# A transformer pair on one core: the router's product on four column groups, high parts multiplied before low parts behind each norm, weight splits and root tables moved out of the norms

## The chip, the cores and the metric

The kernel runs on one core of a Trainium2 chip. The core has a matrix engine (TensorE, PE in the profile; its weight loads are PEld), a vector engine (VectorE, DVE), a scalar engine with function tables (ScalarE, ACT), a general engine (GpSimd, POOL) and a sync engine that issues transfers (SyncE, SP). The engines run their own instruction streams and meet by semaphores. The metric is the device time of one execution in microseconds.

## What is computed

All arithmetic is in float32, on 512 tokens of width 1024. Two blocks follow one another; cut to what matters:

```python
# first block
h = rms_norm(x, norm_mix_g);  z = h @ w_in            # queries, keys, values, gates
x = x + (sigmoid(g_a) * (fox_attention(...) @ w_fox_up)
         + sigmoid(g_b) * (nsa_attention(...) @ w_nsa_up)) @ w_out
t = rms_norm(x, norm_ffn_g)
g_logits = t @ w_group + b_group                       # 4 groups of experts
e_logits = t @ w_router + b_router                     # 16 experts
# best group, its two best experts, their weights; then
x = x + sum_e w_e * (silu(t @ w_gate[e]) * (t @ w_up[e])) @ w_down[e]
# second block
x = x + 0.5 * rms_norm(swiglu(rms_norm(x)), ffn1_post_g)
z = rms_norm(x, mix_pre_g) @ w_in_2                    # neighbourhood and latent attention
x = x + rms_norm(concat(rms_norm(o_na), rms_norm(o_mla)) @ w_out_2, mix_post_g)
x = x + 0.5 * rms_norm(swiglu(rms_norm(x)), ffn2_post_g)
# rms_norm(x, g) = x / sqrt(mean(x*x) + 1e-6) * g
```

## The kernel before

**Split products.** A large float32 product is computed as three products of rounded parts. ACT copies a tile of weights to its high part (`split_high`, line 402), DVE subtracts that from the tile to get the low part (`split_low`, line 408), and PE runs high by high, high by low and low by high (`products`, lines 417 to 419) into one bank of PSUM. The weights come in units of 1 MB; unit `u` lies in buffer `u % 2`, SP loads unit `u` when `split_low` of unit `u - 2` is done, and the first units of the stages have the names AT_FFN1, AT_MID and AT_FFN2 (plus one for the second unit). There are 48 products in each of them.

**A norm and what follows it.** The five norms of the residual (numbers 0 to 4 below: at the start, before the router, before the first FFN, before the second block's attention, before the second FFN) all have the same chain, and everything after waits for it:

1. ACT squares the four tiles of 128 tokens and sums along the row (`norm_squares`, line 1403; after an FFN or an output projection there is first a norm of the result, `post_squares`, line 1417).
2. DVE turns sums into variances (line 1663), ACT takes the root (`root`, line 1394), DVE inverts it (line 1669) and scales the four tiles (line 1683, `harea`; or lines 1698 and 1700 for a norm of a result).
3. PE transposes each tile, 32 blocks in all (`to_features`, line 973), into eight half banks.
4. ACT copies each half bank to the high part `hT_hi` (`to_hT`, line 1411), DVE subtracts for the low part `hT_lo` (`low_features`, line 1711).
5. PE waits for the last low part (`hT_low_ready`) and starts on the first unit.

A root needs another function table than exponent, silu or tanh; the load stands in ACT's stream as ACT_TABLE_LOAD, just ahead of the first instruction that needs it, and does not wait for that instruction's semaphores.

**The order is written by hand**, engine by engine. Around the norms the splits of the next two units stand between the steps: behind the MoE, `split_low(AT_FFN1)` stands ahead of the variance and `split_low(AT_FFN1 + 1)` ahead of the low parts; `split_low(AT_MID + 1)` and `split_low(AT_FFN2)` ahead of the variance of norms 3 and 4; `split_low(AT_FFN2 + 1)` ahead of the low parts of norm 4.

**The router** (line 1137) is plain float32: for each tile of 128 tokens and each of 8 chunks of features, the chunk of `hT` is the stationary operand (128 by 128) and 20 columns of `w_route` move through it. A float32 product is two weight loads and two MATMULs in the trace, so these 32 products are 64 records. DVE then chooses experts, PE counts tokens, DVE makes lists of rows, and POOL gathers the first rows, behind which the expert stage starts.

## Time and profile before

| | us |
|---|---|
| runs: lowest, median, highest of 3 | 2053.97, 2055.45, 3139.5 |
| the profiled execution | 2055.96 |
| its span, first to last instruction | 2054.1 |
| PE busy, weight loads busy | 1816.5, 1439.0 |
| DVE, ACT, POOL busy | 925.0, 853.1, 294.6 |
| mean granted clock of TensorE | 0.935 of full speed |

PE is busy for 88% of the span, and the chain that ended last lies on PE for 84% of it. So what counts are the places where PE has nothing to do or runs at the lower of its two clock levels (1.2 in place of 2.4 GHz, which the profile gives as 0.50).

### The profile page before, as it was taken

What the parts mean: (1) busy time and instruction counts of PE and PEld (TensorE: products, weight loads), DVE (VectorE), ACT (ScalarE), POOL (GpSimd) and SP (SyncE); (2) the same over time, 40 slices, a digit from 0 to 9 for tenths busy, and PEclk for the clock granted to TensorE, in tenths of its full rate; (3) what the DMA queues carried; (4) which work ended last, traced back from release to release, by engine and by line L of the source; (5) the groups of instructions that cost most, each with busy time, mean ns of one, the idle gap of its engine ahead of it and who ended that gap; (6) DMA issues with size and microseconds to landing.
All of it is one profiled execution on the core that took longest, in us unless ns stands there. A gap on an engine that the chain in (4) does not pass through costs nothing.

```text
span 2054.1 us, 22543 instructions
## 1 busy us (share of the span) xinstructions
PE 1816.5 (88%) x8515; PEld 1439.0 (70%) x8515; DVE 925.0 (45%) x1469; ACT 853.1 (42%) x1348; POOL 294.6 (14%) x374
## 2 busy tenths in 40 slices
PE   5996999999769999939999999696767959999996
PEld 4884666668658888828888887583643748888885
DVE  3446334334359999942322323525243352322324
ACT  3224565552348888832223222324456132223221
POOL 2100442220001111200000000623236000000000
PEclk9998899999779999969999999897789979999998
DMA  5223101115369999642324332331010113324321
GB/s 178 97 75 107 48 22 57 47 42 217 131 220 375 387 382 379 225 164 82 102 73 112 92 102 73 103 110 52 1 41 1 52 52 103 102 81 114 85 100 52
DMA packets 160930, 248.37 MB, mean 121 GB/s; under 512 B 11490, under 2 KB 117057, under 8 KB 147904
## 3 DMA queue, kind: packets, MB, share of 16 engines
q1 hardware_dynamic: 151056, 230.21, 33.2%
q0 software_dynamic: 9776, 16.86, 2.7%
q8 instruction: 62, 1.02, 0.2%
q14 instruction: 36, 0.29, 0.0%
HBM read 241.22 MB, written 12.61 MB: 124 GB/s over the span
## 4 chain that ended last, share of the span: by engine, by line
PE 84%; DVE 8%; issue 2%; ACT 2%; POOL 2%; DMA 2%; SPq 0%; DVEq 0%; ACTq 0%
PE psum L417 24%; PE psum L419 23%; PE psum L418 23%; PE psum L553 3%; PE psum L571 3%; PE psum L542 2%; POOL arena L660 2%; DVE tarea_r L1711 1%; DMA warea<-in_w_in 1%; DVE harea L1683 1%; ACT warea_r L402 1%; PE psum L1161 1%; DVE harea L1698 1%; DVE xarea L1700 1%; PE psum L1071 1%
## 5 line engine op out<-in xcount | busy, mean ns | idle before, releaser
L408 DVE TENSOR_TENSOR warea_r<-warea,warea_r 128x2048 fp32r<-128x2048 f32 x114 | 266.5, 2339 | 409.0 <-ACT warea_r L402 408.9
L417 PE MATMUL psum<-tarea_r,warea_r 128*128 128x512 f32 x896 | 358.3, 400 | 13.4 <-DVE tarea_r L1711 13.4
L418 PE MATMUL psum<-tarea_r,warea_r 128*128 128x512 f32 x896 | 352.6, 394 | 0.0
L419 PE MATMUL psum<-tarea_r,warea_r 128*128 128x512 f32 x896 | 352.2, 393 | 0.0
L402 ACT ACTIVATE warea_r<-warea 128x2048 fp32r<-128x2048 f32 x114 | 217.5, 1910 | 287.0 <-PE psum L419 282.6
L417 PE MATMUL psum<-warea_r,arena_r 128*128 128x512 f32 (+1 forms) x768 | 300.7, 392 | 12.1 <-DVE arena_r L2010 7.3
L419 PE MATMUL psum<-warea_r,arena_r 128*128 128x512 f32 (+1 forms) x768 | 297.1, 387 | 0.0
L418 PE MATMUL psum<-warea_r,arena_r 128*128 128x512 f32 (+1 forms) x768 | 297.0, 387 | 0.0
L417 PEld LDWEIGHTS psum<-tarea_r,warea_r 128*128 128x128 f32 x896 | 170.5, 190 | 54.5 <-DVE tarea_r L1711 14.1
L419 PEld LDWEIGHTS psum<-tarea_r,warea_r 128*128 128x128 f32 x896 | 170.5, 190 | 36.4
L418 PEld LDWEIGHTS psum<-tarea_r,warea_r 128*128 128x128 f32 x896 | 170.7, 190 | 33.9
L1573 ACT ACTIVATE arena<-psum 128x512 f32<-128x512 f32 x44 | 26.3, 599 | 370.2 <-PE psum L419 370.2
L417 PEld LDWEIGHTS psum<-warea_r,arena_r 128*128 128x128 f32 (+1 forms) x768 | 143.6, 187 | 44.0 <-DVE arena_r L2010 7.9
L419 PEld LDWEIGHTS psum<-warea_r,arena_r 128*128 128x128 f32 (+1 forms) x768 | 143.3, 187 | 29.3
L418 PEld LDWEIGHTS psum<-warea_r,arena_r 128*128 128x128 f32 (+1 forms) x768 | 143.6, 187 | 28.1
L2057 DVE TENSOR_TENSOR arena<-psum,arena 128x512 f32<-128x512 f32 x44 | 30.4, 692 | 290.4 <-ACT arena L1573 290.4
L417 PE MATMUL psum<-warea_r,tarea_r 128*128 128x512 f32 (+3 forms) x408 | 156.7, 384 | 1.4 <-DVE tarea_r L2126 1.4
L418 PE MATMUL psum<-warea_r,tarea_r 128*128 128x512 f32 (+3 forms) x408 | 155.8, 382 | 0.0
L419 PE MATMUL psum<-warea_r,tarea_r 128*128 128x512 f32 (+3 forms) x408 | 155.7, 382 | 0.0
L973 PE MATMUL psum<-const,harea 128*128 128x128 f32 x160 | 29.2, 368 | 86.6 <-DVE harea L1683 86.6
L660 POOL TENSOR_SCALAR arena<-arena,rr 128x256 f32<-128x256 f32 (+1 forms) x64 | 78.8, 1242 | 122.5 <-DVE rr L583 122.3
L635 ACT ACTIVATE harea<-psum 128x128 f32<-128x128 f32 (+4 forms) x192 | 73.6, 419 | 48.7 <-PE psum L542 48.0
(291 smaller groups left out, 2438.5 us busy)
## 6 DMA issues: line engine op xcount, KB each, us to landing
warea<-in_ffn_w_gu SPq DMA_DIRECT2D x88, 512.0 KB, 5.0
warea<-in_w_in SPq DMA_DIRECT2D x48, 512.0 KB, 4.6
warea<-in_ffn_w_down SPq DMA_DIRECT2D x40, 512.0 KB, 4.2
arena<-in_w_up SPq DMA_DIRECT2D x16, 1024.0 KB, 7.6
tarea<-in_w_up SPq DMA_DIRECT2D x16, 1024.0 KB, 7.1
tarea<-in_w_down SPq DMA_DIRECT2D x16, 1024.0 KB, 7.6
warea<-in_w_gate SPq DMA_DIRECT2D x14, 1024.0 KB, 7.5
harea<-in_w_gate SPq DMA_DIRECT2D x14, 1024.0 KB, 7.8
```

What stands on the lines that cost most here:

```text
L402: act.activation(w_hi[:, u % 2, :], raw[:, u % RAW, :], ACT.Copy).then_inc(s["split_hi"], 1)
L408: dve.tensor_tensor(w_lo[:, u % 2, :], raw[:, u % RAW, :], w_hi[:, u % 2, :].bitcast(f32), ALU.subtract)\
L417: nc.tensor.matmul(out, high, by_high, start=first, stop=False)
L418: nc.tensor.matmul(out, high, by_low, start=False, stop=False)
L419: return nc.tensor.matmul(out, low, by_high, start=False, stop=last)
L542: mm = nc.tensor.transpose(bank[0:rows, P * j:P * j + P], pbuf[:, c0:c0 + rows], ident)
L553: mm = nc.tensor.matmul(ps[st["e"]][:, a:b], st["lhsT"], rhs, start=True, stop=not (mask and b == n))
L571: mm = nc.tensor.matmul(half(bank, e_)[:, c:d_], lhsT, PT[0:lhsT.shape[0], e_, j, a:b], start=start, stop=stop)
L635: nc.scalar.activation(PT[0:rows, st["e"], 0:nj, st["dst"]:st["dst"] + P], src, ACT.Copy)\
L660: ins = nc.gpsimd.tensor_scalar(p, p, rr[:, k:k + 1], None, ALU.mult)
L973: mm = nc.tensor.transpose(ps[2 * t + half_][:, P * c:P * c + P], hn[:, t, P * (4 * half_ + c):P * (4 * half_ + c) + P], ident)
L2057: V.tensor_tensor(sgb[:, v % 2, :], ps[2 * (v % 2) + 1], sgb[:, v % 2, :], ALU.mult).then_inc(s["gated"], 1)
```

## The change

Four things change, and no loop or tiling of the large products does.

- **Router.** The roles are exchanged: the 128 by 20 chunk of `w_route` is stationary and all 512 tokens of `hT` move through it. Chunk `c` writes to partitions 32 * (c % 4) up to 20 more, a column group of the array each, so 8 products leave four partial sums of the logits in one bank. ACT copies the bank (`logit4`), and 4 products with a constant matrix `fold` (a one where partition % 32 equals the column) add the four parts and turn tokens back to partitions. PE waits there for the table of constants too (`list_in`).
- **High parts first.** `products_in_parts` runs the two products that need only `hT_hi` for all parts of the first unit (32 of 48 MATMULs), then waits for the low parts, then runs the other 16. It waits for the high parts and, bank by bank, for the low part that was read from that bank. It is used for the first unit behind norms 0, 2, 3 and 4. A small transposition (line 982) moves behind the first unit of norm 0.
- **Splits** ("halvings") of first and second units move ahead of the norm chain or behind the low parts.
- **Root tables.** `warm()` takes a root of a constant one just before the squares, so that the table is loaded there. The first one waits for the constants (`const_in`), since it reads them.

```diff
+    def products_in_parts(parts, low_ready, complete):
+        for out, pairs, features_first, ready in parts:
+            ready()
+            for n, ((a_hi, a_lo), (b_hi, b_lo)) in enumerate(pairs):
+                nc.tensor.matmul(out, a_hi, b_hi, start=n == 0, stop=False)
+                nc.tensor.matmul(out, *((a_hi, b_lo) if features_first else (a_lo, b_hi)), start=False, stop=False)
+        low_ready()
+        last = []
+        for out, pairs, features_first, _ in parts:
+            for n, ((a_hi, a_lo), (b_hi, b_lo)) in enumerate(pairs):
+                mm = nc.tensor.matmul(out, *((a_lo, b_hi) if features_first else (a_hi, b_lo)), start=False, stop=complete and n == len(pairs) - 1)
+            last.append(mm)
+        return last
     def half(ap, h):
...
             pe.wait_ge(s["const_in"], 16)
             to_features(0)
-            pe.wait_ge(s["hT_low_ready"], 8)
-            pe.wait_ge(s["pos_in"], 32)
-            nc.tensor.transpose(ps[7][:, 0:32], pos_raw, ident[0:32, 0:32]).then_inc(s["pos_psum"], 1)
             def project(n, cols):
                 for h in range(2):
                     u = 2 * n + h
                     pe.wait_ge(s["split_lo"], u + 1)
+                    if u == 0:
+                        def tile_ready(t):
+                            pe.wait_ge(s["ht_ready"], 2 * t + 1)
+                            pe.wait_ge(s["hT_low_ready"], t + 1)
+
+                        parts = [(ps[t][:, 0:cols], [((hT_hi[:, c, P * t:P * t + P], hT_lo[:, c, P * t:P * t + P]),
+                                                      weights(u, cols * c, cols)) for c in range(4)], True,
+                                  lambda t=t: tile_ready(t)) for t in range(NT)]
+                        products_in_parts(parts, lambda: pe.wait_ge(s["hT_low_ready"], 8), False)[-1].then_inc(s["unit_done"], 1)
+                        pe.wait_ge(s["pos_in"], 32)
+                        nc.tensor.transpose(ps[7][:, 0:32], pos_raw, ident[0:32, 0:32]).then_inc(s["pos_psum"], 1)
+                        continue
                     for t in range(NT):
                         j = 4 * n + t
                         if h == 0 and j >= 4:
...
+            for c in range(KD):
+                j = 32 * (c % 4)
+                mm = nc.tensor.matmul(ps[0][j:j + 20, :], w_route[:, c, :], hT[:, c, :], start=c < 4, stop=c >= 4)
+            mm.then_inc(s["route4_psum"], 1)
+            pe.wait_ge(s["list_in"], 16)
+            pe.wait_ge(s["route4"], 1)
             for t in range(NT):
-                for c in range(KD):
-                    mm = nc.tensor.matmul(ps[0][:, 20 * t:20 * t + 20], hT[:, c, P * t:P * t + P], w_route[:, c, :],
-                                          start=c == 0, stop=c == KD - 1)
+                mm = nc.tensor.matmul(ps[3][:, 20 * t:20 * t + 20], logit4[:, P * t:P * t + P], l_("fold"), start=True, stop=True)
             mm.then_inc(s["route_psum"], 1)
...
+                    if g % 2 == 0 and isinstance(v, int) and v == 0:
+                        norm = (2, 4)[g // 2]
+                        parts = [(ps[k], [(weights(u, 1024 * k + P * c, P), (hT_hi[:, c, :], hT_lo[:, c, :])) for c in range(KD)],
+                                  False, lambda k=k: pe.wait_ge(s["hT_low_ready"], low0 + k + 1)) for k in range(2)]
+                        pe.wait_ge(s["ht_ready"], 8 * norm + 8)
+                        products_in_parts(parts, lambda: pe.wait_ge(s["hT_low_ready"], low0 + 8), True)[-1].then_inc(s["unit_done"], 1)
+                        return
...
+                    if u == AT_MID:
+                        pe.wait_ge(s["ht_ready"], 32)
+                        parts = [(ps[r], [(weights(u, cols * c + P * r, P), (hT_hi[:, c, :], hT_lo[:, c, :])) for c in range(4)],
+                                  False, lambda r=r: pe.wait_ge(s["hT_low_ready"], 16 + r + 1)) for r in range(4)]
+                        products_in_parts(parts, lambda: pe.wait_ge(s["hT_low_ready"], 24), False)[-1].then_inc(s["unit_done"], 1)
+                        continue
...
+            def warm():
+                if warmed[0]:
+                    act.wait_ge(s["warm"], warmed[0])
+                else:
+                    act.wait_ge(s["const_in"], 16)
+                warmed[0] += 1
+                nc.scalar.activation(idle, one_col, ACT.Sqrt).then_inc(s["warm"], 1)
             def norm_squares(k):
...
+                if k != 3 and k != 4:
+                    warm()
...
             def post_squares(evacuated):
+                warm()
                 for t in range(NT):
...
             to_hT(1)
+            act.wait_ge(s["route4_psum"], 1)
+            nc.scalar.activation(logit4, ps[0], ACT.Copy).then_inc(s["route4"], 1)
             act.wait_ge(s["exp_in"], 1)
...
             split_high(AT_FFN1)
+            split_high(AT_FFN1 + 1)
             norm_squares(2)
-            split_high(AT_FFN1 + 1)
             to_hT(2, hT_hi)
...
+            split_high(AT_FFN2)
             post_squares(lambda t: 16 + 4 + t + 1)
-            split_high(AT_FFN2)
+            split_high(AT_FFN2 + 1)
             norm_squares(4)
-            split_high(AT_FFN2 + 1)
             to_hT(4, hT_hi)
...
+            split_low(AT_FFN1)
+            split_low(AT_FFN1 + 1)
             for t in range(NT):
...
-            split_low(AT_FFN1)
             norm_rows()
             free_gain(12)
-            split_low(AT_FFN1 + 1)
             low_features(2)
...
             post_norm(0.5)
-            split_low(AT_MID + 1)
             norm_rows()
             free_gain(16)
             low_features(3)
+            split_low(AT_MID + 1)
...
+                else:
+                    split_low(AT_FFN2)
...
             post_norm(1.0)
-            split_low(AT_FFN2)
             norm_rows()
             free_gain(20)
+            low_features(4)
             split_low(AT_FFN2 + 1)
-            low_features(4)```

What that does to the order of instructions is shown at three places. On ACT at the start of the program (norm 0), before and with the change; `harea,ss<-xarea` are the squares, `small<-const` is the root of the constant, `rstd` the root of the variances, `warea_r` a weight split, `tarea_r` the high parts:

```order
L1403 ACT_TABLE_LOAD
L1403 ACTIVATE harea,ss<-xarea 128x1024 [waits x_in] x4
L1394 ACT_TABLE_LOAD
L1394 ACTIVATE rstd<-rstd 128x4 [waits var_ready]
L402 ACTIVATE warea_r<-warea 128x2048 [waits raw0]
L1411 ACTIVATE tarea_r<-psum 128x4x128 [waits ht_psum] x8
```

```order
L1451 ACT_TABLE_LOAD
L1451 ACTIVATE small<-const 128x1 [waits const_in]
L1462 ACTIVATE harea,ss<-xarea 128x1024 [waits x_in] x4
L1439 ACTIVATE rstd<-rstd 128x4 [waits var_ready]
L405 ACTIVATE warea_r<-warea 128x2048 [waits raw0]
L1470 ACTIVATE tarea_r<-psum 128x4x128 [waits ht_psum] x8
```

The load between squares and root is gone, and the squares now stand behind an instruction that waits for the constants. On PE at the router, before and with the change (`const,harea` are the last transpositions of norm 1, `arena,const` the counting of tokens behind the choice of experts):

```order
L973 MATMUL psum<-const,harea 128x128 x7
L1137 MATMUL psum<-w_route,tarea 128x20 [waits route_in,ht_ready]
L1137 MATMUL psum<-w_route,tarea 128x20 x31
L1143 MATMUL psum<-arena,const 128x16 [waits chosen]
L1143 MATMUL psum<-arena,const 128x16 x3
```

```order
L994 MATMUL psum<-const,harea 128x128 x7
L1167 MATMUL psum<-tarea,w_route 20x512 [waits route_in,ht_ready]
L1167 MATMUL psum<-tarea,w_route 20x512 x7
L1172 MATMUL psum<-arena 128x20 [waits route4,list_in]
L1172 MATMUL psum<-arena 128x20 x3
L1177 MATMUL psum<-arena,const 128x16 [waits chosen]
```

32 short products became 8 long ones and, behind a wait for ACT, 4 short ones. On DVE from the last sum of the expert stage to the low parts of norm 2, before and with the change (`xarea` is the residual, `warea_r` a weight split, `tarea_r` the low parts):

```order
L2042 SCALAR_TENSOR_TENSOR xarea<-tarea,arena,xarea 128x1024 [waits y_used]
L408 TENSOR_TENSOR warea_r<-warea,warea_r 128x2048 [waits split_hi]
L1663 TENSOR_SCALAR rstd<-ss 128x4 [waits sumsq]
L1669 RECIPROCAL rstd<-rstd 128x4 [waits root_ready]
L1683 SCALAR_TENSOR_TENSOR harea<-xarea,rstd,garea 128x1024 [waits gain_in0,dve_step]
L1683 SCALAR_TENSOR_TENSOR harea<-xarea,rstd,garea 128x1024 x3
L1690 MEMSET nmax 128x1 [waits hn_ready]
L408 TENSOR_TENSOR warea_r<-warea,warea_r 128x2048 [waits split_hi]
L1711 TENSOR_TENSOR tarea_r<-psum,tarea_r 128x4x128 [waits ht_ready] x8
```

```order
L2106 SCALAR_TENSOR_TENSOR xarea<-tarea,arena,xarea 128x1024 [waits y_used]
L1725 TENSOR_SCALAR rstd<-ss 128x4 [waits sumsq]
L1731 RECIPROCAL rstd<-rstd 128x4 [waits root_ready]
L1745 SCALAR_TENSOR_TENSOR harea<-xarea,rstd,garea 128x1024 [waits gain_in0,dve_step]
L1745 SCALAR_TENSOR_TENSOR harea<-xarea,rstd,garea 128x1024 x3
L1752 MEMSET nmax 128x1 [waits hn_ready]
L1773 TENSOR_TENSOR tarea_r<-psum,tarea_r 128x4x128 [waits ht_ready] x8
```

Both splits have left this stretch; they stand ahead of the sums over the experts' outputs, where DVE waits for a transfer.

## Rows read from the trace of the kernel before

**Rows 1.** Waits of PE, whole span: who waited for whom, total us, times, longest.

```profile
PE psum L973 <- DVE harea L1683: 86.6, 5, 27.1
PE psum L417 <- DVE tarea_r L1711: 13.4, 3, 5.5
```

**Rows 2.** The start: the constants' transfer (size, us to landing), timeline of ACT, DVE, PE.

```profile
const<-in_consts SPq DMA_DIRECT2D x1, 1556.5 KB, 13.7
...
11.85 1.06 ACT L1403 ACTIVATE harea<-xarea 128x1024 f32<-128x1024 f32 x1 [9.85 <-DMA xarea<-in_x]
...
17.88 4.88 DVE L1683 SCALAR_TENSOR_TENSOR harea<-xarea,rstd,garea 128x1024 f32<-128x1024 f32 x4
26.11 4.87 DVE L1711 TENSOR_TENSOR tarea_r<-psum,tarea_r 128x512 fp32r<-128x512 f32 x8
...
31.04 0.31 PE L982 MATMUL psum<-const,arena 32*128 32x32 f32 x1 [5.09 <-DVE tarea_r L1711]
```

**Rows 3.** Timeline: norm 1 with its table load, a norm of a result without one.

```profile
532.24 1.28 ACT L1394 ACT_TABLE_LOAD   x1
...
533.98 4.87 DVE L1683 SCALAR_TENSOR_TENSOR harea<-xarea,rstd,garea 128x1024 f32<-128x1024 f32 x4
...
1649.16 0.19 ACT L1417 ACTIVATION_READ_ACCUMULATOR arena<-harea 128x1 f32 x1
...
1650.04 1.28 DVE L1698 SCALAR_TENSOR_TENSOR harea<-harea,rstd,garea 128x1024 f32<-128x1024 f32 x1
```

**Rows 4.** PE timeline: router, counting; column pairs of attention; one long float32 product, twice.

```profile
542.46 12.28 PE L1137 MATMUL psum<-w_route,tarea 128*128 128x20 f32 x64 [0.74 <-ACT tarea L1411]
559.72 1.89 PE L1143 MATMUL psum<-arena,const 128*128 128x16 f32 x8 [4.99 <-DVE arena L1934]
...
231.88 2.37 PE L571 MATMUL psum<-harea,arena 128*64 128x512 f32 x16
...
199.10 2.07 PE L1071 MATMUL psum<-arena,const 8*128 8x512 f32 x2 [0.38 <-DVE small L1828]
...
240.80 1.12 PE L1071 MATMUL psum<-arena,const 8*128 8x512 f32 x2
```

**Rows 5.** Timeline around norm 2.

```profile
903.13 1.28 ACT L1394 ACT_TABLE_LOAD   x1
...
904.87 4.87 DVE L1683 SCALAR_TENSOR_TENSOR harea<-xarea,rstd,garea 128x1024 f32<-128x1024 f32 x4
909.79 2.29 DVE L408 TENSOR_TENSOR warea_r<-warea,warea_r 128x2048 fp32r<-128x2048 f32 x1
...
916.92 0.79 PE L417 MATMUL psum<-tarea_r,warea_r 128*128 128x512 f32 x1 [5.41 <-DVE tarea_r L1711]
```

**Rows 6.** Timeline around norm 3.

```profile
1294.27 0.19 ACT L1403 ACTIVATION_READ_ACCUMULATOR harea<-xarea 128x1 f32 x1
...
1296.05 4.87 DVE L1683 SCALAR_TENSOR_TENSOR harea<-xarea,rstd,garea 128x1024 f32<-128x1024 f32 x4
...
1302.02 2.07 ACT L1411 ACTIVATE tarea_r<-psum 128x512 fp32r<-128x512 f32 x4 [0.26 <-PE psum L973]
...
1305.89 0.79 PE L417 MATMUL psum<-tarea_r,warea_r 128*128 128x512 f32 x1 [2.54 <-DVE tarea_r L1711]
```

**Rows 7.** Stretches: busy us (count) by engine, clock, DMA share, GB/s; page's clock in 40 slices.

```profile
31.00:35.00 4.00, 3.96 (x10) 3.13 (x11) 2.66 (x4) 0.00 (x0) 0.00 (x0) 0.50 0.14 18
...
544.30:554.00 9.70, 9.70 (x48) 9.70 (x47) 0.00 (x0) 0.00 (x0) 0.00 (x0) 0.50 0.00 0
...
909.50:911.50 2.00, 2.00 (x19) 1.77 (x17) 1.96 (x3) 1.94 (x5) 0.53 (x1) 1.00 0.10 14
...
917.00:922.90 5.90, 5.90 (x14) 4.64 (x15) 0.00 (x0) 0.00 (x0) 0.00 (x0) 0.50 0.10 27
...
1305.90:1308.70 2.80, 2.80 (x7) 2.22 (x8) 0.00 (x0) 0.00 (x0) 2.80 (x6) 0.50 0.22 48
...
PEclk9998899999779999969999999897789979999998
```

21 lines of the change are left out of this document (11 added, 10 removed).

## Prediction

> **What bounds the kernel now.** I read the shares of busy time first, then PE's waits, then the stretches around each norm engine by engine. PE sets the time: 1816.5 of 2054.1 us busy. Its waits say where the rest can be had. The two kinds that the change touches are the wait of the transpositions (line 973) for the scaled rows, 86.6 us in 5 places, and that of the first product behind a norm (line 417) for the low parts, 13.4 us in 3 places [rows 1]; at the start the same wait stands at line 982 with 5.09 us [rows 2]. Most of the 86.6 us are sums, squares and scalings that the change leaves alone. Beside the waits there is a cost that no list of waits shows: after each of them PE works at the lower clock for some us [rows 7]. So I price each norm as a chain with one end, the first large product, and the clock behind it by itself.
>
> **Root tables.** In norm 1 the last square ends where the table load starts, at 532.24, and scaling starts at 533.98: 1.74 us. In a norm of a result where the table was there already, the sum is read at 1649.16 + 0.19 = 1649.35 and scaling starts at 1650.04: 0.69 us [rows 3]. A hidden load is worth 1.05 us, where ACT is idle ahead of the squares. That holds at norm 1, norm 2 and the last norm of the program, whose chain repeats rows 3. Behind the first FFN ACT is not idle: load and dummy root, some 1.5 us, push the squares back by what they save afterwards, and a split on DVE stood in the way too, so I count 0.2 us. Behind the output projection the table is in place before the change. Norm 1 and the last norm: 1.05 + 1.05 = 2.1 us; norm 2 follows below.
>
> The Trainium skill speaks for more: "ScalarE: Activation LUTs", section "What ACT_TABLE_LOAD costs", puts a drain of about 1.38 us on top of the load's 1.28. Rows 3 show the load's 1.28 us and nothing after it: 1.74 us in all, of which 0.69 is there without it. By the page three removed loads would give some 4 us more.
>
> **The start.** Here the same edit costs. The squares begin at 11.85, when x is in, and scaling at 17.88. The dummy root waits for the constants, which land 13.7 us after their issue at 2.58, so at 16.3 [rows 2]. With 0.2 us for the root, 4.27 us for the squares (11.85 to about 16.12) and 0.69 us, scaling starts at 21.5, which is 3.6 us late; it ends at 26.4. `split_low(0)` follows (2.3 us, to 28.7), then the low parts, which began at 26.11 before and begin at 28.7 now. PE no longer waits for eight of them but for one (0.6 us): first product at 29.4 in place of 31.3 (behind line 982, 31.04 + 0.3). The remaining seven land by 33.6 while PE has 32 products before it. Net gain 1.9 us, bounded by the landing of the constants: by up to 0.7 us later if the 13.7 counts from the end of the issue. The small transposition that moves back costs nothing: what DVE does behind it is the split of the third unit, which ACT does not begin before the first unit is through.
>
> **Router.** Before: 64 records in 12.28 us, about 0.19 each, at half clock for most of it (544.3 to 554: 0.50, PE and weight loads both full) [rows 4, 7]. Now 8 products of 512 columns. One such product, two passes, takes 1.12 us at full and 2.07 at half clock from start to end [rows 4], so a pass takes about 0.43 and 0.85, with 0.3 around. Eight in a row: 7.1 or 14 us. Do column groups run side by side? In attention two groups do: 8 products of 512, 384, 256 and 128 columns for two heads are 16 passes, in a row 2 x 2 x 1280 columns at 0.43 us for 512 = 4.3 us, and they took 2.37 [rows 4], so pairs go together. Four groups are not in the trace. If they do too, 4 steps of a pass: 2.0 us at full, 3.7 at half; if only two, 3.7 or 7.1. I take four at a clock between, 2.9 us, since the nearest row shows no loss for two. Added: ACT's copy of the bank 0.65 us with its handovers, and 4 products with `fold`, 8 records like those of line 1143, 1.89 us (1.0 at full clock) [rows 4]. The wait for `list_in` costs nothing: POOL issues that small load when the mixing ends, ahead of the whole output projection. Sum 2.9 + 0.65 + 1.9 = 5.5 us for 12.3: gain 6.8. Ends: 3.7 us (gain 8.6) and 16.6 us (loss 4.3). The choice of experts, lists, gather and expert stage start earlier by that; SP's loads that wait for `route_psum` move with them, and the later ones wait for slots that PE's progress frees, so the stage moves as a whole.
>
> **Norm 2.** The last square ends at 903.13; scaling started at 904.87, held by table load and split. Now 903.13 + 0.69 = 903.8: gain 1.05. Of the 12.05 us from there to the first product (916.92) the second split took 2.3 us, and the rest was the wait for eight low parts [rows 5]. Norm 3 shows the chain without a split in it: scaling 1296.05, last high part 1302.02 + 2.07 = 1304.09, so 8.0 us after scaling began [rows 6]. Norm 2's transpositions started at once too, so I take 7.85: gain 4.2. The low parts end 10 us after scaling began, behind 32 products of some 7 us (half of the 0.42 each that 14 took in 5.9 us at half clock [rows 7]): hidden by 5 us. Both splits now stand where DVE waits for the experts' outputs. Sum 5.3 us.
>
> **Norm 3.** The sum is read at 1294.46, and scaling could start at 1295.15 in place of 1296.05 without the split: 0.9. First product 8.0 in place of 9.84 us after scaling: 1.8 [rows 6]. With the 0.2 of the table 2.9 us. `split_low(AT_MID + 1)` then lies behind the low parts, still some 8 us ahead of its unit (the first takes 48 products, over 10 us, and DVE is through with low parts and split 2 + 2.3 us after it began); the load of unit AT_MID + 3, which waits for that split on SP, starts 10 us later, two units ahead of its use.
>
> **Norm 4.** It repeats norm 2 (first product 12.0 us after scaling, a split of 2.3 us in each of the two places), but has no table load: 0.9 for the first split, 4.2 for the rest: 5.1 us. The split that moves ahead of the last sums of the projection delays the first two of four, which PE's next tiles cover.
>
> **Clock.** Behind norm 2 PE ran 5.9 us at 0.50 [rows 7], behind norm 4 the same, behind norm 3 2.8 us, at the start 4 us: half of each is lost, 2.95 + 2.95 + 1.4 + 2.0 = 9.3 us. In norm 2 the clock had come back during the transpositions (1.00 from 909.5 on) and was lost again in the idle 5.4 us behind them [rows 7]. Now the gap is 0.5 us (1.7 at the start). I take 6.5 of 7.3 us for the three norms and 1.6 of 2.0 for the start.
>
> Against this stands the Trainium skill, "TensorE: Matmul & The Clock Gate", section "Part 4: PE-mode transpose": transpositions do not count as activity for the clock. The row at 909.5 speaks against that. By the page the whole 8.1 us would stay unpaid, which is the first rival.
>
> **Sum.** Tables 2.1, start 1.9 + 1.6, router 6.8, norms 5.3 + 2.9 + 5.1, clock 6.5: 32.2 us. The profiled execution took 2055.96, so 2023.8; the median of the runs lies 0.5 lower, so 2023.3 us.
>
> **Rivals.**
> 1. *The clock does not hold.* The same idle time goes, but the first products start in a half-clock stretch and pay it in full. Mechanism: products right behind transpositions find the level that these left. For it: at norm 3 the clock rose late and fell again at once [rows 7]. Against: in norm 2 it rose while transpositions ran. Time 2023.3 + 8.1 = 2031.4.
> 2. *Column groups run one after the other*, or in pairs. For it: nothing shows four. Against: pairs overlap fully. 14 + 0.65 + 1.9 = 16.6 us, 11.1 more than forecast: 2034.4; pairs only, some 3 us more: 2026.
> 3. *Removed loads are worth more* (the skill's drain, above), by 4 us: 2019. The rows speak against it.
> 4. *Slower than before.* PE's many long stretches at full clock follow the norms. The router row shows that a fully busy PE can sit at 0.50 for 9.7 us [rows 7]. If the new order (each product followed by one with another stationary operand, and short waits between banks) kept the clock down in the units behind the norms, each us at half clock costs 0.5. It decides at 32.2 / 0.5 = 64 us, 16 us behind each of four norms; at 40 us behind each, 80 us would be lost: 2103. Against: only the 48 products behind each norm change their order, each product had its own weight load before (PEld's counts equal PE's), and the router's row has 20 moving columns where these have 512.
> 5. *More than 2% faster.* 41 us would have to go; the ends of the terms above give 35 at most (router 8.6 for 6.8, clock 9.3 for 8.1). The rest would have to come from the attention stages, where the page's clock row stands at 7 to 9 tenths [rows 7] and shifts of start may turn out luckier.
>
> **How the numbers follow.** Forecast 0.60, rival 1 0.15, rival 2 0.10, rival 3 0.04, rival 5 0.08, rival 4 0.03. The range reaches over rivals 1 to 3 with both clock and column groups partly lost, and down by 11 us for router, clock and drain at their good ends: 2012 to 2039. Faster by over 2% means below 2014.3, which is also about what a measurement of this kernel can tell from no change: 0.09. Slower 0.03, within 0.88.
>
> **What the profile of the changed kernel will show.** Router: 16 records on line 1167 in about 3 us, starts in groups of four; over 6 us is rival 2. First product 8 us after scaling began behind norms 2, 3 and 4, with PE's wait for low parts gone, and 0.69 us between last square and scaling. At the start: squares at 16.5, scaling at 21.5. Clock 1.00 in the first unit; 0.50 there is rival 1. I would be wrong most if the high parts come later than in norm 3, or if the constants land well after 16.3.

## Result and the profile after

The changed kernel takes 2022.93 us (median of 4 runs, 2018.61 to 2026.36), the kernel before 2055.09 beside it: ratio 0.9844, 95% interval 0.982 to 0.9868, 1.6% faster. One of the four executions of the kernel before took 3139.5 us, far from every other one, and has no part in the ratio. The forecast was 2023.3 (2012 to 2039). The profiled execution took 2023.19 us, of which its span is 2021.4.

The best way to read a change in six places is to cut both spans at instructions that both kernels have, and to subtract piece by piece. The cuts are the starts of the scalings and of the first large products behind them, and DVE's first step of the choice of experts. "Forecast" is what the prediction's terms give for a piece.

| from, to | before | after | gain | forecast |
|---|---|---|---|---|
| span's start to first product | 31.28 | 29.48 | 1.80 | 1.9 |
| to scaling, norm 1 | 502.70 | 500.12 | 2.58 | 2.65 |
| to choice of experts | 20.79 | 11.29 | 9.50 | 6.8 |
| to scaling, norm 2 | 350.10 | 349.32 | 0.78 | 1.05 |
| to first product | 12.05 | 8.07 | 3.98 | 4.2 |
| to norm of FFN 1's result | 366.44 | 363.34 | 3.10 | 2.8 |
| to scaling, norm 3 | 12.69 | 11.77 | 0.92 | 0.9 |
| to first product | 9.84 | 7.70 | 2.14 | 1.8 |
| to norm of the projection's result | 344.15 | 345.06 | -0.91 | 1.25 |
| to scaling, norm 4 | 12.69 | 11.77 | 0.92 | 0.9 |
| to first product | 12.04 | 7.98 | 4.06 | 4.2 |
| to norm of FFN 2's result | 366.42 | 362.52 | 3.90 | 3.7 |
| to the end | 12.95 | 12.95 | 0.00 | 0 |
| sum | 2054.14 | 2021.37 | 32.77 | 32.2 |

(The three clock terms of 6.5 us are laid out here over the three pieces behind norms 2, 3 and 4 in proportion.) Two pieces are off by over 2 us, with opposite signs. Each column is one execution, and not every piece repeats: in a second execution of the changed kernel (last experiment) the piece to norm 1 took 501.51 us, the one to the choice of experts 12.05 and the one behind norm 3 342.00, so the gains of these three pieces are uncertain by 1.4, 0.8 and 3 us. The others repeated to 0.3 us.

The page first: span, PE, and the granted clock in 40 slices, to be laid beside the last row of [rows 7].

```profile
span 2021.4 us, 22473 instructions
...
PE 1800.8 (89%) x8475; PEld 1422.2 (70%) x8475; DVE 925.3 (46%) x1469; ACT 853.5 (42%) x1354; POOL 294.5 (15%) x374
...
PEclk9998899999879999979999999896689989999998
```

PE is busy for 15.7 us less than before and idle for 17.0 less: half of the gain is waiting, half is the same products at a higher clock and a cheaper router. Then PE's waits after, in the form of [rows 1] (who waited for whom, total us, times, longest):

```profile
PE psum L994 <- DVE harea L1745: 86.0, 5, 25.9
...
PE psum L432 <- issue: 2.7, 3, 0.9
```

The wait for scaled rows stands where it was, as forecast. The 13.4 us for low parts are gone; what is left ahead of the first product is 0.9 us at each of norms 2, 3 and 4, in which ACT copies the last high part. The start, beside [rows 2], timeline with the engines mixed:

```profile
16.49 0.20 ACT L1451 ACTIVATE small<-const 128x1 f32<-128x1 f32 x1 [14.49 <-DMA const<-in_consts]
16.60 1.04 ACT L1462 ACTIVATE harea<-xarea 128x1024 f32<-128x1024 f32 x1
...
21.53 4.87 DVE L1745 SCALAR_TENSOR_TENSOR harea<-xarea,rstd,garea 128x1024 f32<-128x1024 f32 x4
...
28.65 4.87 DVE L1773 TENSOR_TENSOR tarea_r<-psum,tarea_r 128x512 fp32r<-128x512 f32 x8
...
29.48 0.47 PE L432 MATMUL psum<-warea_r,tarea_r 128*128 128x512 f32 x1
```

The squares wait until the constants are in (16.49; 16.3 was forecast) and scaling begins at 21.53, as worked out; PE's first product comes 1.8 us earlier even so, since it needs one low part and not eight. Norm 1, where a hidden table load shows ([rows 3]), and the router ([rows 4]):

```profile
528.72 0.19 ACT L1462 ACTIVATION_READ_ACCUMULATOR harea<-xarea 128x1 f32 x1
...
529.60 2.48 DVE L1745 SCALAR_TENSOR_TENSOR harea<-xarea,rstd,garea 128x1024 f32<-128x1024 f32 x2
...
537.09 1.91 PE L1167 MATMUL psum<-tarea,w_route 128*20 128x512 f32 x16 [0.90 <-ACT tarea L1470]
...
539.07 0.60 ACT L1573 ACTIVATE arena<-psum 128x512 f32<-128x512 f32 x1 [2.03 <-PE psum L1167]
...
539.82 1.04 PE L1172 MATMUL psum<-arena 128*128 128x20 f32 x8 [0.81 <-ACT arena L1573]
540.89 0.24 DVE L1965 TENSOR_TENSOR arena<-psum,small 128x80 f32<-128x80 f32 x1 [6.30 <-PE psum L1172]
```

From the end of the sum's reading (528.91) to scaling are 0.69 us. The router's 16 records take 1.91 us, copy and fold end 3.8 us after the start, at full clock throughout. Norms 2 and 3 for [rows 5] and [rows 6]: scaling, low parts and first product.

```profile
890.21 1.28 DVE L1745 SCALAR_TENSOR_TENSOR harea<-xarea,rstd,garea 128x1024 f32<-128x1024 f32 x1
...
895.73 4.27 DVE L1773 TENSOR_TENSOR tarea_r<-psum,tarea_r 128x512 fp32r<-128x512 f32 x7
...
898.28 0.47 PE L432 MATMUL psum<-tarea_r,warea_r 128*128 128x512 f32 x1 [0.89 <-issue]
...
1273.39 1.28 DVE L1745 SCALAR_TENSOR_TENSOR harea<-xarea,rstd,garea 128x1024 f32<-128x1024 f32 x1
...
1281.09 0.47 PE L432 MATMUL psum<-tarea_r,warea_r 128*128 128x512 f32 x1 [0.94 <-issue]
```

The low parts behind norm 2 end at 900.0, under the first eight of PE's products. Last the clock in the stretches that answer to [rows 7]: start, router, first units of FFN 1, of the second attention stage and of FFN 2 (from and to, us, busy us with counts of PE, PEld, DVE, ACT and POOL, clock, DMA share, GB/s).

```profile
29.50:36.80 7.30, 7.30 (x33) 6.05 (x33) 6.22 (x8) 2.53 (x3) 0.00 (x0) 1.00 0.44 145
537.00:541.00 4.00, 2.95 (x24) 1.34 (x24) 0.11 (x1) 1.92 (x3) 0.00 (x0) 1.00 0.00 0
...
898.30:910.00 11.70, 11.70 (x52) 9.71 (x53) 1.70 (x3) 1.74 (x3) 0.00 (x0) 1.00 0.02 9
1281.00:1292.00 11.00, 10.91 (x48) 9.11 (x49) 4.38 (x5) 0.00 (x0) 11.00 (x22) 1.00 0.56 145
1646.00:1657.00 11.00, 11.00 (x49) 9.10 (x50) 3.91 (x4) 1.11 (x1) 0.00 (x0) 1.00 0.35 97
```

No first unit runs at half clock any more. What these rows don't tell is why, and why the attention stage got slower by 0.9 us. The experiments are about that.

### The profile page after: what moved, and what is told of

It reads as the page before. It is cut to its first block, busy times and chain, and to the rows that moved or that the text cites. A ratio compares the mean times of both kernels' runs of the same rounds, so it can differ in the third digit from the quotient of the medians.

```text
span 2021.4 us, 22473 instructions
## 1 busy us (share of the span) xinstructions
PE 1800.8 (89%) x8475; PEld 1422.2 (70%) x8475; DVE 925.3 (46%) x1469; ACT 853.5 (42%) x1354; POOL 294.5 (15%) x374
## 3 DMA queue, kind: packets, MB, share of 16 engines
q8 instruction: 62, 1.02, 0.2%
## 4 chain that ended last, share of the span: by engine, by line
PE 85%; DVE 7%; ACT 2%; issue 2%; POOL 2%; DMA 1%; SPq 0%; DVEq 0%; ACTq 0%
PE psum L420 23%; PE psum L422 22%; PE psum L421 22%; PE psum L574 3%; PE psum L592 3%; PE psum L563 2%; POOL arena L681 2%; PE psum L994 1%; ACT warea_r L405 1%; PE psum L432 1%; PE psum L1195 1%; DVE harea L1760 1%; DVE xarea L1762 1%; PE psum L433 1%; PE psum L438 1%
## 5 line engine op out<-in xcount | busy, mean ns | idle before, releaser
L411 DVE TENSOR_TENSOR warea_r<-warea,warea_r 128x2048 fp32r<-128x2048 f32 x114 | 266.4, 2339 | 401.0 <-ACT warea_r L405 401.0
L405 ACT ACTIVATE warea_r<-warea 128x2048 fp32r<-128x2048 f32 x114 | 217.4, 1910 | 282.6 <-PE psum L422 261.7
L420 PE MATMUL psum<-tarea_r,warea_r 128*128 128x512 f32 x848 | 336.1, 396 | 0.0
L422 PE MATMUL psum<-tarea_r,warea_r 128*128 128x512 f32 x848 | 331.2, 391 | 0.0
L421 PE MATMUL psum<-tarea_r,warea_r 128*128 128x512 f32 x848 | 331.1, 390 | 0.0
L420 PEld LDWEIGHTS psum<-tarea_r,warea_r 128*128 128x128 f32 x848 | 159.7, 188 | 38.0 <-issue 5.3
L422 PEld LDWEIGHTS psum<-tarea_r,warea_r 128*128 128x128 f32 x848 | 159.7, 188 | 33.8
L421 PEld LDWEIGHTS psum<-tarea_r,warea_r 128*128 128x128 f32 x848 | 159.9, 189 | 31.5
L420 PE MATMUL psum<-warea_r,tarea_r 128*128 128x512 f32 (+3 forms) x392 | 149.8, 382 | 1.4 <-DVE tarea_r L2188 1.4
L421 PE MATMUL psum<-warea_r,tarea_r 128*128 128x512 f32 (+3 forms) x392 | 149.0, 380 | 0.0
L422 PE MATMUL psum<-warea_r,tarea_r 128*128 128x512 f32 (+3 forms) x392 | 149.0, 380 | 0.0
L994 PE MATMUL psum<-const,harea 128*128 128x128 f32 x160 | 28.5, 362 | 86.0 <-DVE harea L1745 86.0
```

Of the source, the lines that this page charges most:

```text
L405: act.activation(w_hi[:, u % 2, :], raw[:, u % RAW, :], ACT.Copy).then_inc(s["split_hi"], 1)
L411: dve.tensor_tensor(w_lo[:, u % 2, :], raw[:, u % RAW, :], w_hi[:, u % 2, :].bitcast(f32), ALU.subtract)\
L420: nc.tensor.matmul(out, high, by_high, start=first, stop=False)
L421: nc.tensor.matmul(out, high, by_low, start=False, stop=False)
L422: return nc.tensor.matmul(out, low, by_high, start=False, stop=last)
L994: mm = nc.tensor.transpose(ps[2 * t + half_][:, P * c:P * c + P], hn[:, t, P * (4 * half_ + c):P * (4 * half_ + c) + P], ident)
```

## Experiments

Each edit is made to the changed kernel unless it says otherwise; times are medians beside runs of the kernel before on the same chip (2055.6 to 2055.8).

### The old router

```diff
-            for c in range(KD):
-                j = 32 * (c % 4)
-                mm = nc.tensor.matmul(ps[0][j:j + 20, :], w_route[:, c, :], hT[:, c, :], start=c < 4, stop=c >= 4)
...
+            for t in range(NT):
+                for c in range(KD):
+                    mm = nc.tensor.matmul(ps[0][:, 20 * t:20 * t + 20], hT[:, c, P * t:P * t + P], w_route[:, c, :],
+                                          start=c == 0, stop=c == KD - 1)
```

> The changed kernel with its old router: 32 products with 20 moving columns, no copy, no fold. Theory: the changed kernel's router took 3.85 us (537.04 to 540.89) where the old one took 12.3, of which 9.7 us were at half clock although PE was fully busy. If these narrow products bring the half clock with them, the old router costs 12 us here too and the time rises by 8.5 us to about 2031.4. Rival: the half clock there was left over from what stood ahead (its phase), and at full clock the 64 records take some 6.5 us: the time rises by 2.7 us to about 2025.6, and the gain of the column groups was mostly one of the clock's luck.

2026.71 us (2025.21 to 2036.9). By the time alone the rival would have won. The trace says otherwise; the router's line, then its two halves as stretches (clock in the third column from the right):

```profile
535.47 10.28 PE L1167 MATMUL psum<-w_route,tarea 128*128 128x20 f32 x64 [0.90 <-ACT tarea L1466]
...
535.50:539.40 3.90, 3.90 (x35) 3.90 (x36) 0.00 (x0) 1.22 (x1) 0.00 (x0) 1.00 0.00 0
539.50:545.70 6.20, 6.20 (x30) 6.13 (x29) 0.00 (x0) 0.00 (x0) 0.00 (x0) 0.50 0.00 0
```

The clock does fall to 0.50 within the narrow products here too, with PE full before and after, only 4 us after their start and not 1.8 as before. They take 10.3 us, 6.4 more than the new router, and the piece from scaling of norm 1 to the choice of experts is 17.94 us for 11.29. Of these 6.65 us the profiled execution gives 1.4 back in the second piece of the table (498.70 for 500.12) and 3.1 behind norm 3 (341.95 for 345.06), pieces that the edit does not touch, and 0.3 at the start. So both theories were half right: the router's gain is 6.5 to 8.5 us, by where the clock falls in the old one, and a difference of 2 us in the total can hide 6.6 in a stage.

### The router alone, on the kernel before

The kernel before with the new router, copy and fold, and nothing else of the change (the same lines as in the change's diff).

> The kernel before with the new router alone (four column groups, copy, fold), nothing else. Theory: 3.85 us at full clock in place of 12.3 to 10.3, 6.5 to 8.5 us less, 2047 to 2049; all of it comes through to the end, since the expert stage moves as a whole. Rival: the expert stage waits for its loads and takes part of it back, under 4 us less.

2048.34 us, ratio 0.9966 (0.9953 to 0.9979), 7.4 us less: as the theory has it. Its line takes 1.91 us again, and the stretch from the choice of experts to norm 2 keeps its length (350.00 for 350.10), so nothing is taken back by the loads of the expert stage. This trace holds a second finding. Behind norm 3 the old order of products and the old waits stand, PE was idle for 3.17 us ahead of the first product, and the clock stayed at 1.00 (it fell there in the kernel before, with 2.54 us). The piece behind took 346.32 us all the same, for 344.15 with the clock lost.

### Two column groups, and one

```diff
-                j = 32 * (c % 4)
+                j = 32 * (c % 2)
```

The second kernel has `c % 1`; `start` and `stop` follow, and the fold runs over 64 and 32 partitions.

> The changed kernel with the router's 8 products on two column groups (chunk c writes to group c % 2) and the fold over 64 partitions. Theory, that the groups run side by side and a product by itself takes two passes of some 0.43 us at full clock: 8 steps of a pass in place of 4, the line's 16 records take 3.7 us in place of 1.91, from the last high part to the logits 5.7 in place of 3.85. Rival, that the 1.91 us come from the 20 columns of the stationary operand and not from groups: it stays at 1.9.

> The changed kernel with all 8 router products on one column group, one accumulation, fold over 32 partitions. Theory: 16 passes in a row, 7.1 us in place of 1.91, so that copy and fold still leave it 3 us ahead of the old router. Rival: stays at 1.9 (narrow stationary operands are fast by themselves). If it takes over 8, the granted clock in that stretch tells whether half clock did it.

The router's line on two groups, and on one, with a stretch of the latter:

```profile
538.93 3.62 PE L1167 MATMUL psum<-tarea,w_route 128*20 128x512 f32 x16 [0.79 <-ACT tarea L1470]
```

```profile
538.44 7.04 PE L1167 MATMUL psum<-tarea,w_route 128*20 128x512 f32 x16 [0.79 <-ACT tarea L1470]
...
538.50:545.40 6.90, 6.90 (x16) 1.46 (x16) 0.00 (x0) 0.00 (x0) 0.00 (x0) 1.00 0.00 0
```

7.04, 3.62 and 1.91 us: the groups run almost fully side by side, and the narrow stationary operand by itself saves nothing. All three stay at full clock, the one of 7 us too, where the 64 records of products with 20 moving columns lost it 1.8 to 4.2 us after their start. The totals (one execution each, 2026.03 and 2025.56) do not keep the order of the stages.

### Waiting for the low parts again

```diff
                         pe.wait_ge(s["ht_ready"], 8 * norm + 8)
+                        pe.wait_ge(s["hT_low_ready"], low0 + 8)
```

and the same wait for eight low parts behind norms 0 and 3.

> The changed kernel, but behind norms 0, 2, 3 and 4 PE waits for all eight low parts before its first product; order of products, splits, tables and router stay. Idle by the trace of the changed kernel: low parts end 1.7 us behind the first product at norm 2, about 2 at norms 3 and 4, 4 at the start, 9.7 us in all. Theory that the short gap is what keeps the clock: the gap behind the transpositions grows from 0.9 to 2.6 us and more, the first unit runs at 0.50 again for some us, 3 to 9 us on top: 2036 to 2042. Rival, that the clock came back for another reason (removed idle ahead of the transpositions): 2032.7 and clock 1.00 behind the norms.

2036.49 us, 13.6 more than the changed kernel. First products behind norms 2 and 4:

```profile
909.59 0.76 PE L432 MATMUL psum<-tarea_r,warea_r 128*128 128x512 f32 x1 [2.66 <-DVE tarea_r L1777]
...
909.60:912.40 2.80, 2.80 (x7) 2.22 (x8) 0.00 (x0) 0.00 (x0) 0.00 (x0) 0.50 0.03 6
...
1661.25 0.47 PE L432 MATMUL psum<-tarea_r,warea_r 128*128 128x512 f32 x1 [3.01 <-DVE tarea_r L1777]
...
1661.30:1665.00 3.70, 3.70 (x17) 3.03 (x18) 1.89 (x1) 0.00 (x0) 0.00 (x0) 1.00 0.08 20
```

The idle time is as expected: 12.09 us from scaling to first product at the start for 7.95, 10.04, 10.05 and 10.05 behind norms 2 to 4 for 8.07, 7.70 and 7.98, 10.5 us in all, where 9.7 were expected. The rest is mostly clock. It was lost at the start (4.39 us idle) and behind norm 2, not behind norms 3 and 4, although the gaps there are longer than the one behind norm 2 (3.06 and 3.01 us for 2.66): a gap of 2.5 to 3.2 us sometimes costs the clock and sometimes not; 0.9 us did not in any trace. The moved splits by themselves show here too: 10.04 us from scaling to product at norm 2, where the kernel before has 12.05.

### The kernel before, with PE kept busy

```diff
+            def keep_busy(base):
+                for m in range(1, 8):
+                    pe.wait_ge(s["hT_low_ready"], base + m)
+                    for j in range(5 if m < 7 else 3):
+                        nc.tensor.transpose(ps[0][:, P * (j % 4):P * (j % 4) + P], hn[:, 0, P * j:P * j + P], ident)
...
             to_features(2)
+            keep_busy(8)
             pe.wait_ge(s["hT_low_ready"], 16)
```

> The kernel before, all waits as they were, with additional transpositions into a bank that is already read, 5 behind each of the first six low parts and 3 behind the seventh, where PE waited idle for the low parts (start and norms 2, 3, 4); their results are overwritten by the first product. No wait goes, so only the clock can gain. Theory, that the short gap keeps the clock and transpositions count for it: clock 1.00 in the first units, 2.0 + 2.95 + 1.4 + 2.95 = 9.3 us less, 2046. Rival, that transpositions don't count for the clock (as the Trainium skill has it): no change, 2055, clock 0.50 behind the norms.

2048.70 us, ratio 0.9966 (0.9954 to 0.9979): 7.0 us less with more work on PE and every wait in place. Behind norm 2 the additional transpositions run up to the first product, and the stretch that stood at 0.50 in [rows 7] stands at 1.00:

```profile
907.76 3.74 PE L982 MATMUL psum<-const,harea 128*128 128x128 f32 x30
911.56 0.50 PE L417 MATMUL psum<-tarea_r,warea_r 128*128 128x512 f32 x1
...
911.70:917.60 5.90, 5.90 (x26) 4.84 (x27) 0.00 (x0) 0.00 (x0) 0.00 (x0) 1.00 0.06 15
```

The two FFN pieces are 2.84 and 2.82 us shorter than before (363.60 for 366.44 and 366.42), where 2.95 was forecast for a whole loss. This is the clock's share behind these two norms by itself. The total is not: the piece up to norm 1 is 2.86 us shorter (499.84; 2.0 was forecast, and this piece repeats to a few us only), and the one to the choice of experts, in which nothing was added, 2.9 (17.85 for 20.79), because the clock rose sooner and fell later there. Norm 3 gained nothing in this trace: there the transpositions ran over and made the first product 1.0 us later, and the attention stage behind it took 346.99.

The Trainium skill, "TensorE: Matmul & The Clock Gate", section "Part 4: PE-mode transpose", has it that a transposition does not count as busy for the clock in the same way and that the full clock does not engage for it. This trace does not agree: with float32 transpositions in the gaps the clock stayed at 1.00 where it had fallen to 0.50.

### The splits back in their places

ACT and DVE with `split_high` and `split_low` of the first and second units where the kernel before had them; products in parts stay.

> The changed kernel with the splits of the first units back in their old places, all else kept. Theory: ahead of the variance a split costs 1.05 us at norm 2 and 0.9 at norms 3 and 4, since the last square has to be waited for anyway; between scaling and low parts it costs nothing, since the first product waits for the last high part (7.9 us after scaling began) and for one low part, which is there 4.9 + 2.3 + 0.6 = 7.8 us after it: 2.9 us more, 2025.8. Rival, that the moved splits are what the norms gained (4.2 us at norms 2 and 4 each): 11 us more, 2034.

2027.93 us (2024.11 to 2031.06), 5 more than the changed kernel. In the trace the splits account for 2.3 of that: 0.92 us more ahead of norms 3 and 4 each (12.69 for 11.77), 0.5 ahead of norm 2 (349.80 for 349.32, a piece that took 348.26 to 349.90 in eight traces with the same code in it, so this term is not shown), and nothing from scaling to product at norms 2 and 4 (7.95 for 8.07 and 7.98). The theory said 2.9. Norm 3 took 0.86 longer from scaling to product, where no split stands in either kernel: its transpositions ran at half clock for longer. The piece behind it took 346.43. The timeline behind norm 2 shows why the second split is free there:

```profile
893.01 2.29 DVE L411 TENSOR_TENSOR warea_r<-warea,warea_r 128x2048 fp32r<-128x2048 f32 x1
...
895.21 3.07 DVE L1773 TENSOR_TENSOR tarea_r<-psum,tarea_r 128x512 fp32r<-128x512 f32 x5
...
896.04 0.47 PE L432 MATMUL psum<-tarea_r,warea_r 128*128 128x512 f32 x1 [0.99 <-DVE tarea_r L1773]
```

DVE splits until 895.2, makes one low part until 895.8, and PE could not have started before the last high part in any case. The order of the products gives the whole 4 us from scaling to product at norms 2 and 4 whether or not the second split is moved (12.05 to 7.95). Moving the split is worth 2.0 us there only while PE waits for all low parts (12.05 to 10.04, the experiment above), and nothing once it does not. What the moved splits bring in the changed kernel is 0.9 us ahead of norms 3 and 4.

### Without the dummy roots

```diff
             def warm():
+                return
```

> The changed kernel without its dummy roots, so that the table loads stand ahead of the real roots again. Theory: 1.05 us more at norm 1, norm 2 and the last norm, 0.2 behind the first FFN, and at the start 2.8 less: squares at 11.85 in place of 16.60, but the first product then waits for the first unit's low weights (26.1) and one low part, 26.7 in place of 29.5. Sum 0.5 us more, 2023.5: the dummy roots as a whole are worth next to nothing. Rival, that a removed load is worth its drain too (2.4 us each): 4.6 us more, 2027.5.

2024.45 us (2022.46 to 2024.56), ratio 0.9847 (0.983 to 0.9863), 1.5 more than the changed kernel where 0.5 was expected, a difference that the totals can't tell from none. Norm 1:

```profile
525.12 0.19 ACT L1463 ACTIVATION_READ_ACCUMULATOR harea<-xarea 128x1 f32 x1
525.33 1.28 ACT L1439 ACT_TABLE_LOAD   x1
...
527.07 4.87 DVE L1746 SCALAR_TENSOR_TENSOR harea<-xarea,rstd,garea 128x1024 f32<-128x1024 f32 x4
```

From 525.31 to 527.07 are 1.76 us, so 1.07 for the load, and the piece up to the last norm is 1.02 longer (363.54 for 362.52), the one up to the norm behind the first FFN 0.2 (363.55 for 363.34). The start is 2.1 us earlier (first product at 27.36). The loads are worth what rows without them say, and over half of what the other dummy roots bring was lost by the first.

### The start, without waiting for the constants

```diff
-                    act.wait_ge(s["const_in"], 16)
-                warmed[0] += 1
-                nc.scalar.activation(idle, one_col, ACT.Sqrt).then_inc(s["warm"], 1)
+                warmed[0] += 1
+                act.wait_ge(s["warm"], warmed[0])
+                nc.scalar.activation(idle, idle if warmed[0] == 1 else one_col, ACT.Sqrt).then_inc(s["warm"], 1)
...
+            V.memset(idle, 1.0).then_inc(s["warm"], 1)
             norm_rows()
             free_gain(4)
```

> The changed kernel, whose first dummy root reads a column that DVE sets to one at the start, in place of the constants. Theory: squares at 11.85, scaling at 16.8, first product bounded by the first unit's low weights and one low part at 26.7 to 27.4 in place of 29.48 (the kernel without tables had it at 27.4): 2.1 to 2.8 us less, 2020.5, so the wait for the constants is what the start lost. Rival: the clock at the start, with a longer idle time between transpositions and first product, falls again and takes 1 to 3.4 us back: no change.

2022.04 us, ratio 0.9832 (0.9816 to 0.9849): no difference to the changed kernel that these runs can tell. The first product came at 27.20, 2.3 us earlier, but PE was idle for 3.85 us ahead of it, and the stretch behind it ran at half clock:

```profile
27.20 0.47 PE L432 MATMUL psum<-warea_r,tarea_r 128*128 128x512 f32 x1 [3.85 <-DVE tarea_r L1770]
...
24.50:27.20 2.70, 0.00 (x1) 0.03 (x1) 2.70 (x3) 2.70 (x7) 0.00 (x0) 1.00 0.00 0
28.20:31.60 3.40, 3.40 (x10) 2.63 (x9) 3.40 (x7) 1.62 (x1) 0.00 (x0) 0.50 0.76 290
```

The stretch at half clock is 3.4 us long, which gives 1.7 us back, the rival's way. The kernel without dummy roots had nearly the same start and kept the clock at 1.00 behind it:

```profile
27.36 0.47 PE L432 MATMUL psum<-warea_r,tarea_r 128*128 128x512 f32 x1 [3.13 <-DVE tarea_r L1774]
```

The piece up to norm 1 took 503.27 us for 500.12. The 1.4 us beyond the lost clock are no more than the second execution of the changed kernel shows (501.51).

### The same with PE kept busy, and earlier first products

```diff
-                        for c in range(4):
+                        for c in range(4) if k or 2 * t + half_ < 7 else [0, 1, 2, 3] * 5:
...
-                        pe.wait_ge(s["ht_ready"], 8 * norm + 8)
+                        pe.wait_ge(s["ht_ready"], 8 * norm + 7)
...
+                if n == 4:
+                    second_half()
```

on top of the edit above; `second_half` waits for the eighth high part, and norm 3 waits for 31 in place of 32.

> The changed kernel with the first dummy root freed from the constants, 16 repeated transpositions ahead of the last half bank of norm 0 (same result) so that PE has no gap there, and behind norms 2, 3 and 4 the first products waiting for the high parts of their own half of the features only (7 of 8, the eighth is waited for at the fifth pair, or at norm 3 not in this unit). Theory: 2.3 us at the start, this time with the clock kept, 0.4 us at each of the three norms: 3.5 us less, 2019.4. Rival, that the gap of 0.9 us has another cause than the last copy: 2.3 us only at most, 2020.6 or more.

2018.05 us (2014.72 to 2021.85), ratio 0.982 (0.9807 to 0.9833). The changed kernel itself gave 2022.62 and 0.9834 (0.982 to 0.9847) beside it: 4.6 us by the medians, where 3.5 were expected, with intervals that overlap a little. The totals don't separate this from the rival's 2.3 us, but the gaps below do. The start again, then the gap ahead of the first product of norm 2:

```profile
18.67 8.18 PE L996 MATMUL psum<-const,harea 128*128 128x128 f32 x48 [18.67 <-DVE harea L1745]
...
27.07 0.47 PE L434 MATMUL psum<-warea_r,tarea_r 128*128 128x512 f32 x1 [0.23 <-DVE tarea_r L1773]
...
27.10:31.00 3.90, 3.90 (x17) 3.23 (x18) 3.90 (x7) 2.60 (x3) 0.00 (x0) 1.00 0.78 268
...
892.86 0.47 PE L434 MATMUL psum<-tarea_r,warea_r 128*128 128x512 f32 x1 [0.35 <-issue]
```

With 16 repeated transpositions in the gap the clock stayed at 1.00, and the gaps behind norms 2 to 4 sum to 1.2 us for 2.7. From scaling to first product these three norms are 1.0 us shorter in all (7.80, 7.55 and 7.42). This is the fastest version in the study by its median.

### The changed kernel once more

> The changed kernel itself once more, nothing edited, to see which stretches of its trace repeat. Theory, that where the clock changes within the attention stages and the output projection is not fixed by the program: the stretch from the first product to the scaling of norm 1 (500.1 us in the first trace) and from the first product behind norm 3 to the norm of the result (345.0) differ by 1 to 4 us, and the stretches at full clock (norms, FFN: 363.3 and 362.5, scaling to first product 8.1, 7.7, 8.0) repeat to 0.3; the median stays within 2 us of 2022.9. Rival, that the 2.3 us lost in the second attention stage belong to the change: both stretches repeat to 0.5 us.

2022.62 us (2019.25 to 2023.52). Its second attention stage, from first product to the norm of the projection's result, and below it the same stretch of the first trace (columns as in [rows 7]):

```profile
1284.10:1626.10 342.00, 278.64 (x1316) 199.48 (x1316) 125.92 (x351) 140.39 (x290) 111.92 (x130) 0.89 0.18 52
```

```profile
1281.10:1626.10 345.00, 281.63 (x1316) 202.35 (x1316) 126.00 (x350) 140.28 (x290) 112.25 (x131) 0.87 0.18 51
```

The same 1316 products took 3 us less of PE's time at a clock 0.02 higher. The FFN pieces repeat to 0.05 us (363.37 and 362.47), norms to 0.3. The piece up to norm 1 took 501.51 for 500.12. The attention code is the same in all kernels here; over the thirteen traces of this study the piece behind norm 3 lies between 341.95 and 346.99: 344.15, 346.32 and 346.99 in the three kernels with the old order of products, 341.95 to 346.43 in the ten with the new one.

## Why the prediction came out, step by step

- **What bounds the kernel.** Right: the wait for scaled rows stayed at 86 us, and the chains behind the norms gave the rest.
- **Root tables**, 1.05 each: 1.07 at norm 1 and 1.02 at the last norm without the dummy root, so the term holds, and so does the 0.2 behind the first FFN. Norm 2 gave 0.78 with the sums ahead of it, in a piece that took 348.26 to 349.90 us in eight traces with the same code in it. The drain that the Trainium skill adds ("ScalarE: Activation LUTs", section "What ACT_TABLE_LOAD costs") would have made three loads some 4 us dearer, by an estimate from that page. No row here shows it: the kernel without dummy roots was only 1.5 us slower, start included, and rival 3 falls.
- **Start**, 1.9 + 1.6: 1.80 for the first product, and the clock at 1.00 from its start. Of the 2.65 forecast for the piece behind it (clock and table of norm 1) 2.58 came, which is partly luck: in the second execution it was 1.19. The constants' wait cost what was worked out. That it costs 2.1 to 2.3 us of a possible start is measured; taking it away alone returned nothing that the totals show, and 1.7 us of that is the lost clock.
- **Router**, the term that was mis-sized: "four at a clock between, 2.9 us" was 1.91 at full clock, and the fold 1.04 for 1.9; 3.8 us from start to end for 5.5, gain 8.5 for 6.8. The reading that the half clock of [rows 7] would partly stay missed that it came with the narrow products. Another 1.0 us of this piece is the clock rising sooner under the transpositions, which is luck: the second execution took 12.05 us for the piece, 0.8 more. Rival 2 falls: 1.91, 3.62 and 7.04 us for four groups, two and one.
- **Norm 2, 3, 4**, 4.2 + 1.8 + 4.2 from scaling to product and 1.05 + 0.9 + 0.9 ahead: 3.98 + 2.14 + 4.06 and 0.78 + 0.92 + 0.92. The mechanism held, but the prediction gave 2.3 us of the 4.2 to the moved second split. With the splits back the gain of 4.1 us remained; the products on high parts bring it alone.
- **Clock**, 6.5 of 7.3: behind norms 2 and 4 the full amount came (2.84 and 2.82 in the kernel before with PE kept busy). The gap left ahead of the first product was 0.9 us where 0.5 was forecast, and none at the start where 1.7 was. Behind norm 3 the first unit ran at full clock too, but the piece became 0.91 us longer. The step that failed is the one from the first unit to the end of its stage: that the 1.25 us saved would still be seen there. The same piece swings by 3 us between two executions of the changed kernel (345.06 and 342.00), so whether the 1.25 came is not shown either way; the kernel before with the new router kept the clock there and took 2.2 us longer than the kernel before. Rival 1 is refuted for gaps of 0.9 us; its mechanism is real at longer ones (2.54 and 2.66 us lost the clock).
- **Rivals 4 and 5.** The products in their new order ran at 1.00 wherever the gap ahead of them was 0.9 us or less, and the FFN pieces of old and new order at full clock, both with the table load in them, agree (363.60 with PE kept busy, 363.55 without dummy roots), so rival 4 has no place. The attention stages were not luckier.

That the total lay 0.4 us from the forecast is in part chance: 2.7 us more at the router and 2.2 less behind norm 3, and the four executions of the changed kernel lie 8 us apart. What stays open: what sets where the clock changes within the attention stages. It was observed, not steered.

## What to carry to other kernels

Multiply first what is ready first: when a product is split into parts, the order of its terms can cover the making of the late part, and shortening PE's gap below a microsecond pays a second time in the clock. Where a gap can't be closed, harmless work in it may be worth more than it costs (2.8 us behind norms 2 and 4; at norm 3 it made the first product 1.0 us later and no gain showed). And read an edit's effect from the pieces that it touches: here totals of identical code differed by more than some edits were worth.

## What the runs showed of the hardware

- Column groups of the array ran almost fully side by side in float32: 8 products of 512 columns in 7.04, 3.62 and 1.91 us on one, two and four groups, 1.94 and 3.69 times as fast. The Trainium skill, "TensorE: Matmul & The Clock Gate", section "Why this matters for your kernels", tells of 2.38 times for three groups; four column groups by themselves were not in it.
- A fully busy PE lost its full clock under products of 20 moving columns in three kernels (1.8, 4.0 and 4.2 us into them). It fell also 0.3 us behind 32 records of products with one moving column that had kept PE busy for 3.7 us (line 1362, at 1578.6 in the changed kernel). Under the large products of the FFN stages, with 512 moving columns, it stayed at 1.00 once it had risen.
- Transpositions kept the clock at 1.00 across gaps that otherwise lost it.
- Of the idle gaps between transpositions and first product in the thirteen traces, 24 of 0.8 to 1.0 us and one of 1.37 kept the full clock, and all of 3.85 us and more lost it. In between length alone does not decide: 2.54 and 2.66 us lost it, 3.01, 3.06, 3.13 and 3.17 did not.
